# Two more weight slots, norm rows spread by TensorE and a 128-row scatter in the expert stage of a two-block transformer kernel

## The reference, cut to what matters

```python
for l in range(2):
    mix = hybrid_mixer(x, ...)                      # two attentions of 8 heads, then @ w_o
    x = layer_norm(ALPHA * x + mix, ln1_g[l], ln1_b[l])
    ffn = grouped_moe(x, router_w, router_bias, w_gate[l], w_up[l], w_down[l])
    x = layer_norm(ALPHA * x + ffn, ln2_g[l], ln2_b[l])

def grouped_moe(h, router_w, router_bias, w_gate, w_up, w_down):   # 16 experts in 4 groups
    aff = sigmoid(xt @ router_w); biased = aff + router_bias
    # the best group by the sum of its two best experts, then the two best experts in it
    gates = one_hot(e_idx, 16) * (aff / sum of the two)
    act = silu(xt @ w_gate[e]) * (xt @ w_up[e]) * gates            # 1024 -> 512, each expert
    return sum over e of act @ w_down[e]                           # 512 -> 1024
```

## Time and profile before

| what | us |
|---|---|
| median of 3 runs | 1145.16 |
| the 3 runs | 1140.54, 1145.16, 1145.20 |
| the profiled execution | 1142.94 |
| its span, first to last instruction | 1141.1 |

### The profile page before, as it was taken

How to read it: one execution, slowest core, us unless ns; L and a number is a source line. 1 busy time by engine, 2 the same in 40 slices (tenths; PEclk the granted TensorE clock), 3 DMA queues, 4 the chain that set the end, 5 groups by cost and what they waited for, 6 DMA issues and landing times.

```text
span 1141.1 us, 16230 instructions
## 1 busy us (share of the span) xinstructions
PE 1083.8 (95%) x6228; PEld 745.9 (65%) x6228; DVE 565.4 (50%) x1082; ACT 438.4 (38%) x797; POOL 92.2 (8%) x120
## 2 busy tenths in 40 slices
PE   7999998999999999899999999889989999999985
PEld 5898988999998798675344443358867744444332
DVE  5754376767667557747222222274684742222224
ACT  5345455555545345743122111143574521121111
POOL 2200000000000112510000000011252000000000
PEclk9999999999999988999999999999989999999998
DMA  8843255565555333358999999944242999999993
GB/s 293 266 148 112 75 176 191 170 200 165 195 192 174 117 128 114 112 196 352 422 420 421 421 421 421 418 158 125 79 156 72 395 368 421 420 421 421 420 421 129
DMA packets 81717, 294.60 MB, mean 258 GB/s; under 512 B 7268, under 2 KB 40402, under 8 KB 56946
## 3 DMA queue, kind: packets, MB, share of 16 engines
q1 hardware_dynamic: 79168, 287.20, 66.0%
q10 hardware_dynamic: 1682, 4.27, 1.0%
q0 software_dynamic: 800, 2.22, 0.5%
HBM read 292.62 MB, written 1.05 MB: 257 GB/s over the span
## 4 chain that ended last, share of the span: by engine, by line
PE 81%; DVE 8%; DMA 5%; ACT 3%; issue 3%; SPq 0%; DVEq 0%; POOL 0%; ACTq 0%
PE bank L2490 17%; PE bank L2499 9%; PE bank L2021 8%; PE bank L2022 8%; PE bank L2023 8%; DMA moe_w<-in_w_up 5%; PE bank L2082 4%; PE bank L2083 4%; PE bank L2084 4%; PE bank L1946 4%; PE bank L2522 3%; PE bank L2116 3%; PE bank L2477 2%; PE bank L2100 2%; PE bank L2204 1%
## 5 line engine op out<-in xcount | busy, mean ns | idle before, releaser
L1183 DVE TENSOR_TENSOR lo<-raw,hi 128x2048 fp32r<-128x2048 f32 (+3 forms) x78 | 166.9, 2146 | 62.7 <-ACT hi L726 62.4
L726 ACT CAST hi<-raw 128x2048 fp32r<-128x2048 f32 (+3 forms) x78 | 139.5, 1795 | 59.7 <-PE bank L2023 57.4
L1425 DVE TENSOR_TENSOR proj<-bank,proj 64x512 f32<-64x512 f32 x32 | 34.7, 1085 | 197.6 <-PE bank L2512 195.3
L2021 PE MATMUL bank<-hi,xs 128*128 128x512 f32 (+2 forms) x312 | 125.9, 404 | 5.8 <-DVE xs L1217 2.9
L2082 PE MATMUL bank<-xs,hi 128*128 128x256 f32 x448 | 127.8, 285 | 3.6 <-DVE xs L1213 1.5
L2083 PE MATMUL bank<-xs,hi 128*128 128x256 f32 x448 | 126.8, 283 | 0.0
L2084 PE MATMUL bank<-xs,lo 128*128 128x256 f32 x448 | 126.7, 283 | 0.0
L2022 PE MATMUL bank<-hi,xs 128*128 128x512 f32 (+2 forms) x312 | 119.5, 383 | 0.0
L2023 PE MATMUL bank<-lo,xs 128*128 128x512 f32 (+2 forms) x312 | 119.3, 382 | 0.0
L1114 ACT ACTIVATE proj<-bank 64x512 f32<-64x512 f32 x32 | 18.9, 590 | 204.6 <-PE bank L2491 204.6
L2082 PEld LDWEIGHTS bank<-xs,hi 128*128 128x128 f32 x448 | 85.9, 192 | 5.0 <-issue 3.5
(11 more groups left out here) (299 smaller groups left out, 2133.6 us busy)
## 6 DMA issues: line engine op xcount, KB each, us to landing
raw<-in_w_up SPq DMA_DIRECT2D x40, 1024.0 KB, 5.2
raw<-in_w_in SPq DMA_DIRECT2D x28, 1024.0 KB, 5.3
moe_w<-in_w_gate SPq DMA_DIRECT2D x24, 1024.0 KB, 19.0
moe_w<-in_w_up SPq DMA_DIRECT2D x24, 1024.0 KB, 20.4
moe_w<-in_w_down SPq DMA_DIRECT2D x24, 1024.0 KB, 20.2
raw<-in_w_down SPq DMA_DIRECT2D x19, 1024.0 KB, 5.4
raw<-in_w_gate SPq DMA_DIRECT2D x10, 1024.0 KB, 16.0
raw<-in_w_o SPq DMA_DIRECT2D x8, 1024.0 KB, 4.9
```

Of the source, the lines that this page charges most:

```text
L726: nc.scalar.copy(high(n)[:, 0:size], raw[:, n % RING, 0:size]).then_inc(S["hi_done"], 1)
L1183: tt(low(n)[:, 0:size], raw[:, n % RING, 0:size], high(n)[:, 0:size].bitcast(F32), ALU.subtract).then_inc(S["lo_done"], 1)
L2021: mm(out_, lhs_hi, rhs_hi, start=first, stop=False)
```

## The change

Five edits, all in both layers.

1. **Slots.** `wide_a` no longer holds norm rows and becomes the second slot, loaded by SyncE in its turn right after `wide_b`. Slab 0 gets a place outside the rotation, in half 1 of `xg`, and is issued just before the load into `attention_slot`. Slab m >= 1 lies in slot (m - 1) mod 16. ScalarE issues no load any more.
2. **Norm rows.** GpSimd loads the two rows of 1024 numbers into one partition each (`ln_rows`). TensorE spreads them with four products of one row each into the accumulator banks 4 to 7, in the place of `open_acc` and among products with zeros; `kept` reads them there. The first scatter then starts the accumulators itself (`first`) and waits for `ln_scaled`.
3. **Gather order.** `rows_lo(1, 0)` moves behind `slots_of(0)`. Gather steps 0 and 1 first add the three parts that don't need it, then the fourth.
4. **Attention order.** `heads_low(2)` comes after `logits(14)` instead of after `logits(13)`.
5. **Scatter.** Plane c of `expert_out` now holds for the feature half c the high part in 64 partitions and the low part in the other 64. So ScalarE and VectorE have two instructions on 64 partitions each instead of one on 128, and the scatter is 4 products with 128 rows.

```diff
         moe_slots = [wide_b[:]] + ...                 # before; wide_a last
+        first_slot = xg[:, 1].rearrange("p e c s -> p (e c s)")
+        moe_slots = [wide_b[:], wide_a[:]] + [raw[:, i, :] for i in range(RING)]
...
                 def moe_load(m, src):
+                    i = m - 1
                     if m == 0:
+                        return
+                    elif i < AT_RAW:
                         sp.wait_ge(S["turned_a"], 8 * (layer + 1))
...
-                    elif m == GAIN_SLOT:
-                        return
-                    elif m >= MOE_SLOTS:
+                    else:
                         moe_wait(sp, layer, "moe_used", m - MOE_SLOTS + 1)
+                    if i == AT_ATTENTION:
+                        sp.dma_start(first_slot.rearrange("p (k n) -> p k n", k=4), gate_w[0, 0]).then_inc(S["moe_first"], 16)
...
+                    if i == 1:
+                        load(b + L_O + 3, rows_of(A["w_o_2"][layer], 6, 2, 0, D))
...
-                pool.dma_start(ln_gb[:, 0, :], gain.partition_broadcast(P)).then_inc(S["ln_in"], 16)
-                pool.dma_start(ln_gb[:, 1, :], shift.partition_broadcast(P)).then_inc(S["ln_in"], 16)
+                for i, src in enumerate((gain, shift)):
+                    pool.dma_start(ln_rows[32 * i:32 * i + 1, :], src.unsqueeze(0)).then_inc(S["ln_in"], 16)
...
-                    nc.scalar.activation(expert_out[:, 0, :], bank[2][:], ACT.Copy, scale=slot_gate[:, e % 2:e % 2 + 1])\
+                    for c in range(2):
+                        out_high(e % 2, c).then_inc(S["moe_out_high"], 1)
...
-                    if e == 0:
-                        act.wait_ge(S["ln_scaled"], 2 * HALVES * layer + HALVES)
-                        act.dma_start(wide_a[:]..., A["w_down_2"][layer]...[1, 1])
...
+                    rows_ = high_rows[c]
+                    return nc.vector.scalar_tensor_tensor(out=expert_out[low_rows[c], c, :], in0=bank[2][rows_, :],
+                                                          scalar=slot_gate[rows_, at:at + 1],
+                                                          in1=expert_out[rows_, c, :].bitcast(F32),
+                                                          op0=ALU.mult, op1=ALU.subtract)
...
                 pe.wait_ge(S["logits_normed"], HALVES * (layer + 1))
-                open_acc()
-                busy(12, bank[2])
+                pe.wait_ge(S["ln_in"], 16 * (4 * layer + 2))
+                for which in range(2):
+                    for c in range(2):
+                        mm(acc[which][c][:], const[32 * which:32 * which + 1, C_ONE:C_ONE + 1].broadcast_to([1, P]),
+                           ln_rows[32 * which:32 * which + 1, 512 * c:512 * (c + 1)], start=True, stop=True)\
+                            .then_inc(S["gains_spread"], 1)
+                        busy(2, bank[2])
+                busy(2, bank[2])
+                for f in range(2):
+                    mm(bank[f][:], zeros[:], zeros[:, 0:1].broadcast_to([P, 512]), start=True, stop=False)
...
-                        for split_ in range(2):
-                            for c in range(2):
-                                part = slice(SLOTS * c, SLOTS * (c + 1))
-                                ins = mm(acc[half][c][:], slot_to_token[part, at, half * P:(half + 1) * P],
-                                         expert_out[part, split_, :], start=False, stop=False)
+                        ins = mm(acc[half][c][:], slot_to_token[:, at, half * P:(half + 1) * P], expert_out[:, c, :],
+                                 start=first, stop=False)
```

More of the change, by code:

```diff
@@ L342, in build @@
         place = route[:, 3, :]
+        upper, lower = slice(0, SLOTS), slice(SLOTS, P)
+        high_rows, low_rows = (upper, lower), (lower, upper)
         def row_chunks(part, half, i):
@@ L1388, in kept @@
                     part = slice(512 * c, 512 * (c + 1))
[L1389 removed]
+                    nc.vector.scalar_tensor_tensor(out=x[:, half, part], in0=x[:, half, part], in1=bank[4 + c][:],
                                                    scalar=stat[:, 2, half:half + 1], op0=ALU.mult, op1=ALU.mult)\
@@ L1394, in kept @@
                     part = slice(512 * c, 512 * (c + 1))
-                    ins = tt(x[:, half, part], x[:, half, part], ln_gb[:, 1, part], ALU.add)
+                    ins = tt(x[:, half, part], x[:, half, part], bank[6 + c][:], ALU.add)
                 ins.then_inc(S["ln_scaled"], 1)
@@ L2556, in scatter_expert, with gather_parts @@
                 def scatter_expert(e):
+                    if e == 0:
+                        pe.wait_ge(S["ln_scaled"], 2 * HALVES * layer + HALVES)
                     moe_wait(pe, layer, "moe_map_ready", e + 1)
-                    moe_wait(pe, layer, "moe_out_ready", e + 1)
-                    add_out(e % 2).then_inc(S["moe_scattered"], 1)
-                for f in range(4):
-                    if f % 2 == 0:
-                        pe.wait_ge(S["rows_lo"], 2 * HALVES * layer + HALVES + 1 + f // 2)
+                    for c in range(2):
+                        moe_wait(pe, layer, "moe_out_ready", 2 * e + c + 1)
+                        ins = add_out(e % 2, c, first=e == 0)
+                    ins.then_inc(S["moe_scattered"], 1)
+                def gather_parts(f, pairs, stop=False):
+                    for c in range(2):
+                        chunk = slice((2 * f + c) * P, (2 * f + c + 1) * P)
+                        for half, part in pairs:
+                            ins = mm(bank[f][:, c * 256:(c + 1) * 256], x_rows[:, part, half, chunk], one_hot[:, 0, half],
+                                     start=False, stop=stop and c == 1)
+                    return ins
+                moe_wait(pe, layer, "moe_one_hot", HALVES)
+                pe.wait_ge(S["rows_hi"], 2 * HALVES * layer + HALVES + 1)
+                for f in range(2):
+                    gather_parts(f, ((0, 0), (0, 1), (1, 0)))
+                pe.wait_ge(S["rows_lo"], 2 * HALVES * layer + HALVES + 1)
+                for f in range(2):
+                    gather_parts(f, ((1, 1),), stop=True).then_inc(S["moe_gathered"], 1)
+                pe.wait_ge(S["rows_lo"], 2 * HALVES * layer + 2 * HALVES)
+                for f in range(2, 4):
                     if f == 3:
```

102 lines of the change are left out of this document (52 added, 50 removed).

## The result

| | us |
|---|---|
| before, median of 6 runs (range) | 1143.65 (1140.54 to 1145.20) |
| after, median of 6 runs (range) | 1154.49 (1150.84 to 1158.94) |
| ratio, 95% interval | 1.0104 (1.0082 to 1.0125) |
| profiled execution: before, after | 1142.94, 1153.3 |

What follows compares the result with a forecast made beforehand. In the experts the DMA weight stream was taken as the bound, ending last. Per layer -4.0 - 0.4 - 1.2 + 1.3 = -4.3, both -8.6, against 1142.94: 1134.3, forecast 1134.5 us, range 1129 to 1142.

Steps and rivals of the forecast that it cites:

- the start of the experts: From zeros through count to expert 0: later count +0.29 and moved rows_lo(1, 0) +1.05 us, taken +1.3 a layer.
- T: Start of TensorE's count before expert 0: taken 524.2, 523.6 at best, against 523.31 before.
- The price of one product: Before the count, each one-row product was priced at 0.43 us, its pair of weight loads.
- The changes of height: Before the count, eight changes between one-row and full products; at 0.2 us each, T would be 525.2.
- the late start: Rival: mode changes cost 0.2 us or more, count starts at 525.3; -3.2 a layer, 1136.5 us; chance 0.13.
- the lost lead: Rival: load rhythm leaves holes in the expert stream, slab 91 only 0.5 earlier; -0.8 a layer, 1141.3 us; chance 0.11.
- slots: Expert weight stream: two more slabs loaded before first use save 5.0 us, a 0.9 hole gives part back; -4.0 a layer.
- scatter and tail: Scatter 0.19 us shorter an expert; behind slab 91, -0.19 once and -0.07 twice; taken -0.4 a layer.
- attention order: Attention units 14 and 15: TensorE's 1.54 us idle goes, products start at 492.65 instead of 493.89; -1.2 a layer.
- my bound of -3.6: Slots' upper bound a layer: the lone load is also slow at its start and the next ones start slowly again.
- I called the prediction wrong if slab 91 lands less than 3 us nearer: Sign in the expert stream: slab 91 was to land about 195.1 us after expert 0's first product, 199.14 before.
- Count to expert 0: From the start of TensorE's count to expert 0's first product: 6.8 us instead of 6.39.

Runs made afterwards that it cites:

- with 128 rows: The kernel after, with gain and shift spread by products of 128 rows instead of one, in the same order between products with zeros; 1143.19 us, 0.9995 of before.
- the kernel with the late products: The kernel after, with the four one-row products moved back to back behind the count, replacing four products with zeros; 1137.06 us, 0.9942 of before.
- old scatter: The kernel with the late products, with the scatter put back to eight products of 64 rows; 1135.28 us, 0.9932 of before.
- the old order of attention: The kernel with late products, old scatter and rows_lo(1, 0) before the count, with heads_low(2) back beside unit 13; 1139.26 us, 0.9961 of before.
- without the four products: The kernel after, with the four one-row products replaced by four products with zeros into the same banks; 1139.77 us, 0.9958 of before.
- both old: The kernel with the late products, with the old scatter and rows_lo(1, 0) back in front of the count; 1135.62 us, 0.9927 of before.
- with 64 and 32 rows: The kernel after, with gain and shift spread by products of 64 or 32 rows; 1147.52 and 1145.27 us, 1.0046 and 1.0029 of before.

## Why the prediction was wrong

The step that failed is the start of the experts. The prediction put T, the start of the count, 0.9 us later, and the whole at +1.3 (bounds +0.7 and +2.4); measured are +8.5 and +8.3. Its 4.9 us from the zeros to the count starts at 519.32, so from the first zeros it is 5.7, against 12.78. Three things, by the runs:

- The price of one product. I took 0.43 for the pair of instructions, from products back to back. Those overlap with their neighbours. Alone among zeros the pair takes 0.85 to 0.96: with 128 rows the count is 1.9 later than before, with no change of height.
- The changes of height. I put 0.2 each, 1.6 in all, into the late start; the forecast's T lies only 0.6 above the sum without them, and I gave no working for the 0.6. They cost 1.0 for eight.
- The clock. I had a fall of some 5 us at 2.5 in the lost lead, with a share of 0.11. It came in both layers of the profile, for 13.6 us each, and cost 12.78 - 7.74 = 5.0 us before the count in each. That is half of the 20 us by which I missed. In the kernel before, this stretch is filled with full products with zeros, and I did not ask what one-row products among them would do to the clock.

The other terms, a layer:

| term | predicted | measured, layers 1 and 2 |
|---|---|---|
| slots | -4.0 (-5.0 to -3.6) | -3.1 and -2.3; in other kernels, where the count isn't late, -3.2 to -3.9 |
| scatter and tail | -0.4 (-0.8 to +0.1) | +1.4 and +0.5 |
| attention order | -1.2 (-1.5 to -0.8) | -1.35 and -1.13, from the kernel with this edit alone |
| start | +1.3 (+0.7 to +2.4) | +8.5 and +8.3 |
| sum of both layers (their measured terms) | -8.6 | +10.8 (profiled: +10.4) |

**Slots**: the mechanism was right, with a dip behind each of the first two uses in the windows of the kernel with the late products (from 534 to 536 and from 537 to 540; 197, 328, 180, 262 and 385 GB/s). The second dip costs 1.0 us against 421 GB/s, about the 0.9 that I took; the slow restart behind the first use was in my bound of -3.6, not in the -4.0. It stood in the kernel before already: from 535 to 536 DMA moved 287 GB/s there, so that its stream ran from 535.0 and not from 534.7. I called the prediction wrong if slab 91 lands less than 3 us nearer: the first layer of the kernel after passes with 3.1, the second with 2.3 does not, and why it gets 0.8 less isn't known. **Scatter**: on TensorE the 0.19 was right (0.20), and that four full products would cost no less than eight paired ones was not borne out (0.92 against 1.12). But behind slab 91 my terms add up to -0.33, where I took -0.4. I priced ScalarE's half at 0.59, by a row of the same shape with another target; it takes 0.69, and I left out `lo`, queued behind VectorE's second half, which costs about 0.9 in the first layer. **Attention**: right, by the profiles. **Count to expert 0**: 6.88, predicted 6.8, for here the moved instruction costs 0.45.

With the term of the start as it is when the products stand behind the count (+0.3), the sum is 2 x (-1.2 - 3.6 + 0.3 + 0.9) = -7.2, and the kernel with the late products measured -7.1. The best versions, with the old scatter, lie 8 to 9 us below before.

## What to carry to other kernels

Take a price from rows with the same neighbours: an instruction that overlaps with its like back to back can cost double when it stands alone among others. Products with zeros did not hold the clock here once one-row products stood between them; such products belong where TensorE waits anyway, not in front of something that another engine waits for. And when a step is halved in work per instruction, look at what stands queued behind the added instruction.

## What the runs showed of the hardware

- Four float32 products of one row and 512 columns between pairs of bfloat16 products of 128 rows: clock 0.50 for 13.6 us in both layers of the profile, and by their times probably in all six runs. Back to back in front of the same zeros: 3.4 us, and 10.2 in the other layer, where the fall came first. Back to back behind the count, in five kernels with two layers each: in three of the ten stretches (old scatter, layer 2; the old order of attention, both layers) the clock falls behind them for 3.4 us before expert 0 starts. Without one-row products there (before, before with the new attention order, without the four products, and with 128, 64 and 32 rows in front of the count) none of twelve has it. That the products are its cause isn't shown.
- Runs of one kernel differ by up to 9.5 us (with 64 and 32 rows 12 and 14), and tend to lie the lower the higher the mean clock: both old, 1129.1 at 0.981 and 1138.6 at 0.974. The stretches at 0.50 differ from one profiled kernel to the next in number and length, also where the code is the same: in the second layer's stretch from the load into `wide_b` to that into `attention_slot` they last 10.2 and 3.4 us in the kernel after, 6.8 and 3.4 in the one with the late products.
- To write `expert_out`, ScalarE and VectorE take 0.69 and 0.75 us for 512 columns from a bank, with 64 partitions as with 128.
